# Banded attention's row factors through neighbouring-value sums and ScalarE copies, and stick-breaking attention with ScalarE's weights first

## The reference

```
s = where(|qpos - kpos| <= 128, q . k * G_SCALE, -inf)
p = softmax([s_ctx, s_band, sink])           # the sink's share is dropped
o = p_ctx @ v_ctx + p_band @ v_band
```

## Time and profile before

| what | value |
|---|---|
| time, median of 3 runs | 2769.32 us (2768.6 to 2769.61) |
| the profiled execution | 2770.5 us, span 2768.7 us |
| TensorE matmuls | 2566.3 us busy, 93% of the span |
| VectorE, ScalarE, GpSimd | 1419.2, 1153.6, 381.1 us busy |
| granted TensorE clock | 0.969 of full speed, mean |

### The profile page before, as it was taken

How to read it: one execution, slowest core, us unless ns; L and a number is a source line. 1 busy time by engine, 2 the same in 40 slices (tenths; PEclk the granted TensorE clock), 3 DMA queues, 4 the chain that set the end, 5 groups by cost and what they waited for, 6 DMA issues and landing times. The chain is left out here.

```text
span 2768.7 us, 38552 instructions
## 1 busy us (share of the span) xinstructions
PE 2566.3 (93%) x14759; PEld 1979.2 (71%) x14759; DVE 1419.2 (51%) x2283; ACT 1153.6 (42%) x1977; POOL 381.1 (14%) x415
## 2 busy tenths in 40 slices
PE   4999998999999999989999999899998999999787
PEld 3778987877778878933337778786334877798776
DVE  5113265666655514666764723411777547265752
ACT  6112344454454321134443622311767647333662
POOL 1000020010020000046761000000000010004710
PEclk8999999999999999989999999999999999998889
DMA  7430010000112131110002220102000220111012
GB/s 257 174 139 24 18 33 1 1 1 1 62 54 91 47 61 46 32 37 1 1 1 91 92 78 30 59 3 76 1 1 24 84 88 31 38 47 62 1 54 76
DMA packets 87991, 139.73 MB, mean 50 GB/s; under 512 B 19513, under 2 KB 54738, under 8 KB 87682
## 3 DMA queue, kind: packets, MB, share of 16 engines
q1 hardware_dynamic: 70592, 75.90, 8.8%
q0 software_dynamic: 16976, 61.30, 6.2%
q10 hardware_dynamic: 242, 0.07, 0.0%
HBM read 120.47 MB, written 16.78 MB: 50 GB/s over the span
## 5 line engine op out<-in xcount | busy, mean ns | idle before, releaser
L169 ACT ACTIVATE WORK<-PS 128x512 f32<-128x512 f32 (+5 forms) x309 | 152.6, 494 | 659.2 <-PE PS L863 388.7
L863 PE MATMUL PS<-HT_R,W_R 128*128 128x512 f32 (+1 forms) x896 | 334.3, 373 | 0.0
L862 PE MATMUL PS<-WORK_R,W_R 128*128 128x512 f32 (+1 forms) x736 | 271.4, 369 | 0.0
L861 PE MATMUL PS<-WORK_R,W_R 128*128 128x512 f32 (+1 forms) x672 | 250.0, 372 | 14.4 <-DVE W_R L169 9.9
L169 ACT ACTIVATE HT<-PS 128x1024 f32<-128x1024 f32 (+6 forms) x211 | 156.0, 739 | 161.0 <-PE PS L1296 126.4
L989 PE MATMUL PS<-WORK_R,HT_R 128*128 128x512 f32 x528 | 210.3, 398 | 8.8 <-DVE W_R L169 7.5
L863 PE MATMUL PS<-W_R,WORK_R 128*128 128x256 f32 (+3 forms) x704 | 215.2, 306 | 0.0
L990 PE MATMUL PS<-WORK_R,MIXT_R 128*128 128x512 f32 x544 | 214.1, 394 | 0.0
L991 PE MATMUL PS<-W_R,HT_R 128*128 128x512 f32 x528 | 207.4, 393 | 0.0
L862 PE MATMUL PS<-W_R,HT_R 128*128 128x256 f32 (+2 forms) x688 | 206.2, 300 | 0.0
L926 PE MATMUL PS<-BASE,WORK 128*128 128x128 f32 (+1 forms) x1186 | 175.2, 283 | 25.3 <-DVE WORK L169 16.8
(11 more groups left out here) (328 smaller groups left out, 5587.3 us busy)
## 6 DMA issues: line engine op xcount, KB each, us to landing
MIXT<-in_w_mod POOLq DMA_DIRECT2D x8, 2048.0 KB, 8.7
x_scratch<-WORK POOLq DMA_DIRECT2D x24, 512.0 KB, 2.9
WORK<-x_scratch POOLq DMA_DIRECT2D x24, 512.0 KB, 3.6
W<-in_odd_w_in SPq DMA_DIRECT2D x12, 1024.0 KB, 5.2
W<-in_even_w_in SPq DMA_DIRECT2D x5, 2048.0 KB, 7.9
W<-in_w_mod SPq DMA_DIRECT2D x4, 2048.0 KB, 20.8
WORK<-in_x POOLq DMA_DIRECT2D x16, 512.0 KB, 8.7
W<-in_e_w_in SPq DMA_DIRECT2D x6, 1024.0 KB, 5.9
```

The lines of the kernel that those rows point to most:

```text
L169: self.last = Signalled(self, issue(*args, **kwargs))
L861: mm(out, a[0], b_[0], start=k == 0, stop=False)
L862: mm(out, a[1], b_[0], start=False, stop=False)
L863: return mm(out, a[0], b_[1], start=False, stop=k == KT - 1)
```

## The change

- Banded attention. The rows' maximum is kept positive: ScalarE rounds it into ROWS with a copy (`gqa_round`, in step last-2 of a group, behind the weighing), and the sign moves into the constant that spreads the rows (CS_ROWS is minus one). VectorE forms the sink's exponent as the sum of two neighbouring values, the rounded maximum and minus the sink (`gqa_sink_scores`, a TENSOR_REDUCE in step last-1); minus the sink is laid into ROWS (columns 16 to 19) once at the start. ScalarE's exponentials take the scale -G_SCALE, and a third operation writes minus the rounded exponential beside the full one, so that the difference is a TENSOR_REDUCE over neighbours too. The TENSOR_SCALAR, the SCALAR_TENSOR_TENSOR and the small TENSOR_TENSOR of each group are gone.
- `group_low_parts` for the next group moves on VectorE from k = 1, ahead of that step's unit of the maxima, to k = 3, behind it.
- Stick-breaking attention. On ScalarE the weights of block n-2 stand ahead of the exponential of block n, not between it and the logarithm.

```diff
@@ -89,7 +89,7 @@
     for n in range(4):
         stage[:, CS_FOUR + n * P:CS_FOUR + (n + 1) * P] = ((row < 12) & (row % 4 == n))[:, None]
     stage[:, CS_SINKS:CS_SINKS + P] = ((row >= 4) & (row < 12))[:, None] & (half[:, None] == block)
-    stage[:, CS_ROWS:CS_ROWS + P] = (row < 4)[:, None]
+    stage[:, CS_ROWS:CS_ROWS + P] = -1.0 * (row < 4)[:, None]
     g = 1.0 - 2.0 ** (-5.0 - np.arange(RH))
     base[:, CB_QD:CB_QD + RH] = g[None, :] ** (i[:, None] + 1.0)
     base[:, CB_KD:CB_KD + RH] = g[None, :] ** (-(i[:, None] + 1.0)) * RDK ** -0.5
@@ -278,7 +278,7 @@
                                       "sinks_ready", "rows_ready")]
         scored, weighed, valued, summed, totalled, inverted, out_taken, mixed = [
             sem(f"gqa_{n}") for n in ("scored", "weighed", "valued", "summed", "totalled", "inverted", "out_taken", "mixed")]
-        gqa_const_in = sem("gqa_const_in")
+        gqa_const_in, maximum_found, maximum_rounded = [sem(f"gqa_{n}") for n in ("const_in", "maximum_found", "maximum_rounded")]
         z_ready, low_ready, ln_ready, sp_ready, logs_summed, total_ready, weight_ready, decay_out, decayed_acc, block_ready, block_taken = [
             sem(f"stick_{n}") for n in ("z_ready", "low_ready", "ln_ready", "sp_ready", "logs_summed", "total_ready", "weight_ready",
                                         "decay_out", "decayed_acc", "block_ready", "block_taken")]
@@ -723,8 +723,9 @@
         FOUR_ROWS_R = WORK_R[:, 17920:17920 + P]
         SPARE_SUM = [work(13824, 1024), W[:, g_held, 0:1024]]
         psum_of = lambda m: (TABL[:, :] if m % 2 == 0 else SPARE_SUM[m >= 6]).rearrange("p (a c) -> p a c", a=2)
-        TOP, TAIL, SINK_T, SINK_F = [SMX[:, 16 + 8 * n:24 + 8 * n] for n in range(4)]
-        TOP_MAX = TOP
+        TOP_MAX, SINK_PAIR, SINK_T = SMX[:, 16:24], SMX[:, 24:40].rearrange("p (a i w) -> p a i w", a=2, i=4), SMX[:, 40:48]
+        halves_of = lambda rows: rows.rearrange("p (a c) -> p a c", a=2)
+        top_and_sink = lambda rows: halves_of(rows)[:, :, 0:32].rearrange("p a (w i) -> p a i w", w=2)[:, :, 0:4, :]
         TOP_OF = [HT[:, 9088 + 24 * gp:9112 + 24 * gp].rearrange("p (a i w) -> p a i w", a=2, i=4) for gp in range(2)]
         TOPS, GOUT, GSUM = PS[:, 0:1024], PS[:, 3072:3584], PS[:, 3584:4096]
         z_of = lambda n: PS[:, 1024 + 1024 * (n % 2):2048 + 1024 * (n % 2)]
@@ -2018,11 +2019,18 @@
                     ins = f(GQH[m % 3][:, c], raw, ACT.Copy)
                 ins.then_inc(group_high, 1)
 
+            def gqa_round(m):
+
+                act.wait_ge(maximum_found, m + 1)
+                f(halves_of(ROWS_R[m % 2])[:, :, 0:4], heads4(TOP_MAX, 2), ACT.Copy).then_inc(maximum_rounded, 1)
+
             def gqa_sinks(m):
 
                 act.wait_ge(tops_ready, m + 1)
-                f(ROWS_R[m % 2].rearrange("p (a c) -> p a c", a=2)[:, :, 4:8], heads4(SINK_T, 2), ACT.Exp)
-                f(SINK_F, SINK_T, ACT.Exp).then_inc(sinks_ready, 1)
+                high = ROWS_R[m % 2].rearrange("p (a c) -> p a c", a=2)[:, :, 4:8]
+                f(high, heads4(SINK_T, 2), ACT.Exp, scale=-G_SCALE)
+                f(SINK_PAIR[:, :, :, 0], heads4(SINK_T, 2), ACT.Exp, scale=-G_SCALE)
+                f(SINK_PAIR[:, :, :, 1], halves_of(ROWS[m % 2])[:, :, 4:8], ACT.Copy, scale=-1.0).then_inc(sinks_ready, 1)
 
             def gqa_weigh(n):
                 act.wait_ge(scored, 2 * (n + 1))
@@ -2041,6 +2049,7 @@
             nc.scalar.preload_act_table_set(EXP_AND_LN)
             copy_unit(("gqt", NL // 2 - 1, 3), QT2[3][:, NL - 2:NL, :], 512)
             group_high_parts(1)
+            gqa_round(0)
             gqa_sinks(0)
             slabs_done = 0
             for n in range(len(gsteps) + 2):
@@ -2049,6 +2058,8 @@
                     gqa_weigh(n)
                     if k == 0 and m + 2 < len(groups):
                         group_high_parts(m + 2)
+                    if m + 1 < len(groups) and n == last_step[m] - 2:
+                        gqa_round(m + 1)
                     if m + 1 < len(groups) and n == last_step[m] - 1:
                         gqa_sinks(m + 1)
                     if k in (1, 2) and 2 <= m and slabs_done < 2 * KT and (m >= 8 or slabs_done < KT):
@@ -2129,13 +2140,12 @@
                     f(SF[k % 2][:, 0:w], PS[:, 512:512 + w], ACT.Exp, scale=-1.0).then_inc(decay_out, 1)
 
             for n in range(len(blocks) + 2):
+                if n >= 2:
+                    stick_weights(n - 2)
                 if n < len(blocks):
                     e = SE[n % 2][:, :, 0:512 - cols_of(n)]
                     act.wait_ge(low_ready, n + 1)
                     f(e, e, ACT.Exp)
-                if n >= 2:
-                    stick_weights(n - 2)
-                if n < len(blocks):
                     f(e, e, ACT.Ln, bias=1.0).then_inc(ln_ready, 1)
                 if n >= 2:
                     stick_decay(n - 2)
@@ -2779,19 +2789,17 @@
 
                 t, gp = groups[m]
                 parts = TOP_OF[gp] if has_tail(t) else TOP_OF[gp][:, :, :, 0:3:2]
-                v.tensor_reduce(heads4(TOP_MAX, 2), parts, AX_X, ALU.max)
-                rows = ROWS_R[m % 2].rearrange("p (a c) -> p a c", a=2)
                 if m >= 2:
                     dve.wait_ge(tops_filled, 2 * (tops_before["rows", m - 2, 0] + 1))
-                v.tensor_scalar(rows[:, :, 0:4], heads4(TOP_MAX, 2), -1.0, None, ALU.mult)
-                v.scalar_tensor_tensor(heads4(SINK_T, 2), ROWS[m % 2].rearrange("p (a c) -> p a c", a=2)[:, :, 0:4], G_SCALE,
-                                       heads4(SINK[:, 8 * gp:8 * gp + 8], 2), ALU.mult, ALU.add).then_inc(tops_ready, 1)
+                v.tensor_reduce(heads4(TOP_MAX, 2), parts, AX_X, ALU.max).then_inc(maximum_found, 1)
+
+            def gqa_sink_scores(m):
+                dve.wait_ge(maximum_rounded, m + 1)
+                v.tensor_reduce(heads4(SINK_T, 2), top_and_sink(ROWS[m % 2]), AX_X, ALU.add).then_inc(tops_ready, 1)
 
             def gqa_sinks(m):
                 dve.wait_ge(sinks_ready, m + 1)
-                rows = ROWS_R[m % 2].rearrange("p (a c) -> p a c", a=2)
-                v.tensor_tensor(rows[:, :, 8:12], heads4(SINK_F, 2), ROWS[m % 2].rearrange("p (a c) -> p a c", a=2)[:, :, 4:8],
-                                ALU.subtract).then_inc(rows_ready, 1)
+                v.tensor_reduce(halves_of(ROWS[m % 2])[:, :, 8:12], SINK_PAIR, AX_X, ALU.add).then_inc(rows_ready, 1)
 
             def gqa_rows(m):
                 wait_tops(("rows", m, 0))
@@ -2835,8 +2843,10 @@
                     for rows in ROWS:
                         v.memset(rows, 0.0)
                     for gp in range(2):
+                        v.tensor_scalar(halves_of(ROWS[gp])[:, :, 16:20], heads4(SINK[:, 8 * gp:8 * gp + 8], 2), -1.0 / G_SCALE, None, ALU.mult)
                         v.tensor_scalar(TOP_OF[gp][:, :, :, 2], heads4(SINK[:, 8 * gp:8 * gp + 8], 2), 1.0 / G_SCALE, None, ALU.mult)
             gqa_shift(0)
+            gqa_sink_scores(0)
             group_low_parts(0)
             dve.wait_ge(gqa_const_in, 48)
             v.tensor_copy(FOUR_ROWS_R, GPT[0][:, 0:P])
@@ -2849,12 +2859,14 @@
                 m, k = group_of_step(n)
                 for done in after_group(n, 5):
                     gqa_mixed(done)
+                if m is not None and m + 1 < len(groups) and n == last_step[m] - 1:
+                    gqa_sink_scores(m + 1)
                 gqa_tops(n, 0)
                 for done in after_group(n, 1):
                     gqa_out(done)
-                if k == 1 and m + 1 < len(groups):
+                gqa_tops(n, 1)
+                if k == 3 and m + 1 < len(groups):
                     group_low_parts(m + 1)
-                gqa_tops(n, 1)
                 if (m, k) in ((14, 0), (15, 0)):
                     gate_diagonal(m - 14)
                 if k == 3 and m in (12, 13):
```

## The result

| | before | after |
|---|---|---|
| time, median of 4 runs each | 2768.96 us (2767.89 to 2769.61) | 2798.83 us (2786.48 to 2801.47) |
| ratio | | 1.0102, 95% interval 1.0085 to 1.0118 |
| the profiled execution | 2770.5 us, span 2768.7 us | 2797.11 us, span 2795.3 us |
| granted TensorE clock, mean | 0.969 | 0.961 |
| banded stage, first to last transpose of the row factors | 1186.3 to 1446.5: 260.2 us | 1185.9 to 1477.8: 291.9 us |

The changed kernel is 1.0% slower (some 30 us). The banded stage lost 31.7 us and the stick-breaking stage won about 6. TensorE's lines have moved by one: L1349 is the transpose that was L1348, L1338 and L1325 are the maxima, L1297 the scores, L1519, L1522, L1531, L1538 and L1550 the stick-breaking stage's mask, scores, sums, totals and values.

A forecast was written before the change was run, and what follows sets the result against it. TensorE, at work 93% of the span, bounds the kernel; 40 us of its waits can be won. Stick-breaking -13 and banded +8.2 make -4.8: 2765.7 us profiled, 2764.5 us as median; range 2755 to 2770.5.

The forecast's parts named there:

- What comes: Banded stage, subtraction at k = 3: transpose waits 1.8 us behind a single, 2.5 behind two (2.0 or 3.1).
- the banded term: Banded stage as a whole: +8.2 us, between -2.7 and +12, from the subtraction moved to k = 3.
- The rule of the Trainium skill: VectorE: two-SBUF-input instructions are fully blocked by a GpSimd instruction reading SBUF, tensor_reduce never; favours row factors, opposes moved subtraction.
- The row factors: Banded stage, small operations: unblocked VectorE reduces of 0.18 us each, ScalarE copies of 0.21 us each, 6.7 us more, covered.
- Hidden: Banded stage: ScalarE's rounding starts the weighing 0.8 us later per group, which costs nothing because its readers come later.
- The stick-breaking term: Stick-breaking stage: weights ahead of the exponential remove most of the scores' 14.7 us of waits; -13 us, bounds -14.7 and 0.
- Rival (c): Stick-breaking stage: waits of VectorE's gapless stretches return, stage gives 6.5 us, banded +8; 2771 us; chance 0.14.
- rival (b): Stick-breaking stage: later logarithm delays softplus and sums (L1530) by 13.2 us, nothing won; 2777 us; chance 0.09 with blocked reduces.
- Rival (a): Banded stage: the subtraction at k = 3 costs nothing, stick-breaking gain stands; 2755 us; chance 0.27.
- Rival (d): Banded stage: the small reduces are blocked as well, some 2 us more lost a group; chance 2 in 100.
- What would show it: Both stages: list of expected signs in the new profile, namely TensorE's waits by line and durations of VectorE's operations.

The follow-up runs named there:

- run 1: The kernel before with the stick-breaking edit alone (weights of block n-2 ahead of the exponential of block n): 2761.73 us against 2769.5, ratio 0.9975.
- run 3: The kernel before with only the new row factors, low parts left at k = 1, stick-breaking order as before: 2765.05 us, ratio 0.9983.
- run 2: The kernel before with only the queries' low parts moved from k = 1 to k = 3: 2804.23 us, ratio 1.013.
- run 5: The changed kernel with the low parts back at k = 1, so row factors and stick-breaking edit only: 2758.58 us against 2768.86, ratio 0.9966.
- Run 4: The changed kernel plus unread matmuls on constants in TensorE's wait ahead of the transpose in eleven groups: 2781.16 us, ratio to before 1.0042.
- Run 6: The kernel before with the stick-breaking edit and also ScalarE's decay of block n-2 ahead of the logarithm of block n: 2755.81 us, ratio 0.9958.
- run 8: The changed kernel with only single subtractions at k = 3, the pairs back at k = 1: 2772.92 us, ratio to before 1.0013.

## Why the prediction was wrong

The forecast was 2764.5 us, range 2755 to 2770.5, with "slower" at 0.10. It came to 2798.8. The runs put the three edits at -7.8 (run 1), -4.5 (run 3) and +34.7 us (run 2), together +22.4; the whole change lost 30 in its comparison, 26.6 in the profiled execution, with 15 us between its own fastest and slowest run. Two of the edits add up within 2 us (run 5). Most of what is missing from the sum of three is the row factors' gain, which the moved subtraction takes away: from 1186 to 1478 us TensorE stands still 36.3 us with both and 36.9 with the move alone. The pairs' waits fall from 4.00 to 3.13, but the single ones rise from 1.72 to some 1.92, since the single subtraction, unblocked in run 2, now starts just behind an addition. Without that gain the sum is 34.7 - 7.8 = +26.9. The rest is inside the changed kernel's own spread and was not settled.

**The step that failed: "What comes" in the moved subtraction.** It priced a wait of TensorE by its length. The waits came where it put them and for its reason, with the sizes 1.9 where it took 1.8, and 3.13 where it took 2.5 and named 3.1 as the other case: 20.2 us in the middle groups instead of 17.2, so +11.3 where +8.3 was forecast (bound +10.7). Outside them the waits grew by 13.6 - 11.3 = 2.3 us, where 0 was taken (at most +2); there the scores of three groups waited 4.8 us for low parts that now came last (the first two 1.93 and 1.87 us, forecast as 1.6 and 1.9). Waiting alone would have made the banded term +13.6 instead of +8.2, and the time some 2770. What was left out altogether is the 17.4 us that TensorE lost at the lower clock behind these waits. Run 4 shows this by itself: the subtractions in the same place, the clock back at 0.98, and the stage 16.2 us shorter. The profile before had one sign of it that I didn't follow: the last group's transpose waits 2.49 us at 1446.56, and the granted clock of the next 5 us is 0.66, while 1.00 stands behind every wait of 1.0 to 1.4 us from 1210 on.

```profile
1446.56:1451.56 5.00, 5.00 (x16) 1.94 (x18) 0.69 (x1) 1.02 (x1) 2.53 (x2) 0.66 0.02 5
```

The profiled execution was forecast at 2765.7 us and took 2797.11. Of these 31.4 us, 5.4 are longer waits in the banded stage, 17.4 the lower clock, and 6.8 the stick-breaking stage (-6.2 there instead of -13); the other 1.8 us belong to none of the three.

The rule of the Trainium skill that I weighed (SBUF — State Buffer, "Who interferes with whom") held on both sides: 48 reduces of 0.17 to 0.18 us, also while an addition ran, and single subtractions of 1.75 to 1.78 us in the middle groups instead of 0.69. The trace adds a condition that the forecast left out: the subtraction is blocked where GpSimd's addition started first, and in run 2, where it started 0.01 us ahead of the addition, it took 0.69. The rule spoke against this edit; I gave its price to the wait alone.

**The row factors** were right in mechanism and too cheap in size. "Hidden" was right for ScalarE's copies; but freeing VectorE of the blocked operations is worth 4.5 us where the low parts stay at k = 1 (run 3), since the transposes' waits of 1.03 us go, and the forecast gave it no term of its own. Beside the moved subtraction next to nothing of it is left.

**The stick-breaking term** had the right sign and was mis-sized: -13 forecast, -7.8 measured. Rival (c) gave its size (6.5), but not by its mechanism, and rival (b)'s wait at L1530 never came (1.8 us before, 1.6 after, once). A wait did change its place as (b) had it, but to the totals. The forecast followed who waits for the exponential and the logarithm, and forgot the decay behind them, for which the totals wait. Run 6 moves just that and wins the 13 us (13.1).

**Rival (a)**, that the subtraction costs nothing, fell. **Rival (d)** fell too: no reduce was blocked.

**What would show it:** L1348 in the middle groups from 3.7 to about 17 (came: 20.2), L1324 to nothing (came), the subtractions longer than 0.69 and 0.43 (came), reduces of 0.18 (came), L1518 from 13.9 to some 2 (came: 2.1), L1530 none new (came). Each sign came true and the time was wrong by 34 us: the list asked for waits only, never for the clock or for TensorE's busy time.

## What to carry to other kernels

Where TensorE is at work for nine tenths of the time, price a new wait by its length and by the matmuls behind it at the lower clock: here 13.6 us of new waits brought 17.4 us more, and short matmuls on constants in the waits bought nearly all of these back (16.2 us of the stage). A VectorE operation that GpSimd blocks isn't made cheap by moving it late, but by a place where VectorE itself waits for TensorE (2.13 us ahead of the maximum took it whole). Of an engine's reordered loop follow every operation behind the moved one to its readers, also those that only free a place in PSUM.

## What the runs showed of the hardware

**The clock behind a wait.** How long TensorE had stood still, and the granted clock in the 5 us behind it, over the banded stage from 1200 on in the kernel before, the one after, and runs 2, 3 and 8:

| wait | times | clock 1.00 behind it | lower (0.50 to 0.68) |
|---|---|---|---|
| 1.03 to 1.43 us | 29 | 29 | 0 |
| 1.51 to 1.96 us | 24 | 11 | 13 |
| 2.49 to 4.19 us | 12 | 0 | 12 |

The first class is not safe everywhere. These kernels have one more wait of 1.35 to 1.41 us at 1193 to 1196, 9 to 10 us behind the first transpose's wait of 4.1 us, and there the clock behind it was 0.66 or 0.67 in three of the five (before, runs 2 and 3). In the middle class waits of the same length went both ways within one execution (run 8), so the length alone doesn't decide there; what does stays open. It may also be behind the spread of the changed kernel (2786 to 2801 us, while run 3 stays within 1.9 us): its fastest execution has a mean granted clock of 0.968, the other three 0.960 or 0.961. That was not tried further.

The clock comes back by itself: in run 8 all of 1323 to 1350 us is at 1.00 again, so each long wait pays anew.

**Who is blocked.** In five groups of run 2 a single subtraction starts 0.01 to 0.06 us ahead of a GpSimd addition, takes its 0.69 us, and the addition takes 1.76 to 1.80 us instead of 1.26. In the four middle groups of the changed kernel it starts 0.03 to 0.06 us behind the addition and takes 1.75 to 1.78 us. A few hundredths of a microsecond decide which engine pays.
